# Expert outputs put back by matmuls and summed in SBUF; model dimension in blocks of 512 for the mixture of experts

## What is computed

```
g_val, g_idx = lax.top_k(g_prob, 1)            # one of 4 groups
e_val, e_idx = lax.top_k(e_prob, TOP_K)        # two of its 8 experts
weights = g_val * e_val                        # e_val normalised to sum 1
...
a = jnp.einsum('td,edf->tef', t, w1)
b = jnp.einsum('td,edf->tef', t, w3)
hid = jax.nn.silu(a) * b * cw[:, :, None]
y = jnp.einsum('tef,efd->td', hid, w2)
...
x = x + gt_f * rms_norm(y, g_post_ffn)
```

## Time and profile before

| | |
|---|---|
| median of 3 runs | 1644.57 us (1641.36 to 1647.06) |
| the profiled execution, its own time | 1643.16 us |
| its span in the trace | 1641.3 us |
| first hidden pass starts | 655.94 us |
| last output pass starts | 1604.09 us |
| busy: PE / DVE / ACT / POOL | 72% / 32% / 10% / 8% of the span |
| moved by DMA | 601.0 MB, 366 GB/s over the span |

### The profile page before, as it was taken

How to read it: one execution, slowest core, us unless ns; L and a number is a source line. 1 busy time by engine, 2 the same in 40 slices (tenths; PEclk the granted TensorE clock), 3 DMA queues, 4 the chain that set the end, 5 groups by cost and what they waited for, 6 DMA issues and landing times.

```text
span 1641.3 us, 21098 instructions
## 1 busy us (share of the span) xinstructions
PE 1181.2 (72%) x8541; PEld 597.1 (36%) x8542; DVE 522.5 (32%) x861; ACT 159.5 (10%) x395; POOL 132.4 (8%) x239
## 2 busy tenths in 40 slices
PE   1649999999999997865465465564664669698471
PEld 1538854675445445321122121221221223233120
DVE  4558246565475624212112111121121122223114
ACT  3101121221011011000000000000000000000002
POOL 3000000000010000100100001001001011111102
PEclk8679999899999997978778787787787789899786
DMA  9989869688768977799999999999999998999994
GB/s 301 308 315 380 299 237 354 227 321 312 292 242 320 408 312 308 307 425 433 424 428 426 426 431 425 426 433 423 426 432 425 431 425 341 396 385 407 422 424 189
DMA packets 99964, 601.00 MB, mean 366 GB/s; under 512 B 7736, under 2 KB 18152, under 8 KB 61536
## 3 DMA queue, kind: packets, MB, share of 16 engines
q1 hardware_dynamic: 90352, 571.49, 85.4%
q0 software_dynamic: 7808, 20.85, 4.0%
q10 hardware_dynamic: 1776, 8.28, 1.4%
HBM read 583.28 MB, written 17.32 MB: 366 GB/s over the span
## 4 chain that ended last, share of the span: by engine, by line
PE 52%; DMA 36%; DVE 5%; SPq 4%; issue 2%; ACT 1%; POOL 0%; POOLq 0%; ACTq 0%; DVEq 0%
DMA stream<-in_w 32%; PE ps L586 12%; PE ps L741 11%; PE ps L669 7%; PE ps L758 5%; PE ps L712 5%; PE ps L508 4%; DMA stream<-in_w_ada 3%; PE ps L583 3%; SPq L395 2%; PE ps L537 1%; DVE wk L1075 1%; SPq L400 1%; SPq L455 1%; DVE acc L795 1%
## 5 line engine op out<-in xcount | busy, mean ns | idle before, releaser
L741 PE MATMUL ps<-stream,wk 128*32 128x256 f32 x4608 | 310.7, 437 | 281.8 <-DMA stream<-in_w 280.3
L741 PEld LDWEIGHTS ps<-stream,wk 128*32 128x32 f32 x4608 | 164.0, 126 | 441.6 <-issue 366.7
L1069 DVE COPY wk<-ps 128x512 f32<-128x512 f32 x36 | 24.9, 692 | 778.0 <-PE ps L712 778.0
L586 PE MATMUL ps<-stream 128*128 128x512 f32 x448 | 200.5, 603 | 0.0
L758 PE MATMUL ps<-stream,wk 128*32 128x512 f32 x1152 | 137.3, 618 | 48.8 <-DVE wk L1079 48.6
L712 PE MATMUL ps<-resid,wr 128*32 128x512 f32 x592 | 133.4, 1030 | 2.1 <-DVE wr L1039 2.1
L586 PEld LDWEIGHTS ps<-stream 128*128 128x128 f32 x448 | 85.2, 194 | 100.9 <-issue 100.7
L669 PE MATMUL ps<-stream 128*128 128x512 f32 x256 | 112.8, 603 | 1.3 <-issue 1.3
L508 PE MATMUL ps<-stream 128*128 128x256 f32 x448 | 106.9, 404 | 4.1 <-DMA stream<-in_w_in 2.3
L508 PEld LDWEIGHTS ps<-stream 128*128 128x128 f32 x448 | 91.2, 205 | 18.0 <-DMA stream<-in_w_in 2.7
L1387 POOL COPY wk<-wk 128x512 f32<-128x512 f32 x35 | 21.5, 613 | 803.9 <-ACT wk L1295 803.9
(11 more groups left out here) (236 smaller groups left out, 805.7 us busy)
## 6 DMA issues: line engine op xcount, KB each, us to landing
stream<-in_w SPq DMA_DIRECT2D x128, 2048.0 KB, 25.6
stream<-in_w SPq DMA_DIRECT2D x32, 4096.0 KB, 33.1
stream<-in_w_ada SPq DMA_DIRECT2D x72, 1024.0 KB, 5.7
stream<-in_w_in SPq DMA_DIRECT2D x8, 4096.0 KB, 16.4
stream<-in_w_ada SPq DMA_DIRECT2D x12, 2048.0 KB, 20.4
stream<-in_w_out SPq DMA_DIRECT2D x4, 4096.0 KB, 18.4
stream<-in_w_in SPq DMA_DIRECT2D x3, 3584.0 KB, 23.1
ys<-wk POOLq DMA_DIRECT2D x140, 64.0 KB, 6.3
```

The source lines that it names most:

```text
L586: last = nc.tensor.matmul(bank(fill % 2), hT[:, k, P * half:P * half + P], w[:, k, :], start=(k == 0), stop=(k == KD - 1))
L741: last = nc.tensor.matmul(bank(1)[32 * g:32 * g + 32, 0:256], xe[:, k, :], a13[g // 2][:, k, 256 * (g % 2):256 * (g % 2) + 256], start=(k ...
L1069: V.tensor_copy(xp, bank(0)).then_inc(rows_sb, 1)
```

## The change

**No `ys`.** The writes to HBM, the zeroing, the gather, the gate and sum steps at the end, and POOL's loop are gone. Instead DVE makes from the same 0/1 matrices the gate-weighted ones (`gated`, then `fours`: the 32 columns repeated four times), PE transposes them (two transposes, bank 0), ACT copies them to `spread`, and `add_part(t2, b0)` multiplies `spread` with `ye`: four matmuls with 32 contraction rows each, partition group g of `spread` and `ye` into bank b0+g, all 128 tokens by 512 columns. There are two such calls per tile, one per token half. DVE's `collect` adds the four banks (128 x 2048) to the running sum `ysum[t2]` in SBUF. The sum of tile t-1 is made during tile t; the last one after the loop. Both calls in the loop use banks 4 to 7, so the second waits until DVE has collected the first (`ysum_sb`).

**Order of the model dimension.** For the experts and the router it is split as (g p j): four blocks g of 512, partition p holding dimensions 512g + 4p to 512g + 4p + 3. `pick_rows` now reads x1 in contiguous blocks of 512, `turn_rows` reads every fourth float, and w1 and w3 come in four runs of 8 KB per partition, w3's halves in two. `mod_sums` for m = 3 and 4 takes every 4th float instead of every 16th. The small vectors and router weights are loaded to match: nine more DMAs on POOL's queue at the start.

**`g2b`** is loaded behind the last w2, after the loop, into the buffer of w1.

```diff
-        w1 = a["w1"].rearrange("l e (p k) f -> (l e) p (k f)", p=P)
-        w3 = a["w3"].rearrange("l e (p k) f -> (l e) p (k f)", p=P)
+        w1 = a["w1"].rearrange("l e (g p j) f -> (l e) p g (j f)", g=4, p=P)
+        w3 = a["w3"].rearrange("l e (g p j) f -> (l e) p g (j f)", g=4, p=P)
...
-            sp.wait_ge(g2_out, 16)
-            sp.wait_ge(x1_sq, TT)
-            sp.dma_start(g2b, row_bcast(gdram[1, :, :], D)).then_inc(g2_in, 16)
...
+            sp.wait_ge(g2_out, 16)
+            done = sp.value_load(cums[0:1, NE - 1:NE], min_val=1, max_val=MAX_TILES)
+            sp.wait_ge(ab_ps, done)
+            sp.dma_start(g2b, row_bcast(gdram[1, :, :], D)).then_inc(g2_in, 16)
...
+                    cols = slice(512 * (k // 4) + k % 4, 512 * (k // 4) + 512, 4) if m in (3, 4) else slice(k, D, KD)
...
-                        last = nc.tensor.matmul(bank(0)[32 * g:32 * g + 32, :], pick[:, t2, :], rows[:, t2, 4 * g:4 * g + 4, :], start=(t2 == 0), stop=(t2 == TT - 1))
+                        last = nc.tensor.matmul(bank(0)[32 * g:32 * g + 32, :], pick[:, t2, :], resid[:, t2, 512 * g:512 * g + 512], start=(t2 == 0), stop=(t2 == TT - 1))
...
+            def add_part(t2, b0):
+
+                for g in range(4):
+                    last = nc.tensor.matmul(ps[:, b0 + g, :], spread[32 * g:32 * g + 32, t2, :], ye[32 * g:32 * g + 32, :], start=True, stop=True)
+                last.then_inc(part_ps, 1)
...
-                    last = nc.tensor.transpose(bank(4, 4, P)[:, j, :], xp[:, P * j:P * j + P], ident)
+                    last = nc.tensor.transpose(bank(3, 4, P)[:, j, :], xp[:, j::4], ident)
...
+                        pe.wait_ge(ye_sb, t + 1)
+                        pe.wait_ge(ysum_sb, 2 * t + 2)
+                        add_part(0, 4)
                         pe.wait_ge(pick_sb, t + 2)
                         pick_rows()
...
+                        pe.wait_ge(ysum_sb, 2 * t + 3)
+                        add_part(1, 4)
                         pe.wait_ge(rows_sb, t + 2)
+                        pe.wait_ge(gated_sb, t + 1)
+                        for t2 in range(TT):
+                            last = nc.tensor.transpose(bank(0, 4, P)[:, t2, :], wrf[:, 320 + P * t2:320 + P * t2 + P], ident)
+                        last.then_inc(spread_ps, 1)
                         turn_rows()
...
+            add_part(0, 4)
+            add_part(1, 0)
...
+            def gate_hits():
+
+                return V.tensor_tensor(gated, hit, gates[:, :, :].rearrange("p t j -> p (t j)").unsqueeze(2).to_broadcast((P, 2 * TT, ROWS)), ALU.mult)
+
+            def gate_rows():
+                return V.tensor_tensor(fours, gated[:, 0::2, :].unsqueeze(2).to_broadcast((P, TT, 4, ROWS)),
+                                       gated[:, 1::2, :].unsqueeze(2).to_broadcast((P, TT, 4, ROWS)), ALU.add)
+
+            def collect(t2, b0):
+
+                y4 = ysum[t2].rearrange("p (g n) -> p g n", g=4)
+                V.tensor_tensor(y4, ps[:, b0:b0 + 4, :], y4, ALU.add).then_inc(ysum_sb, 1)
...
-            with pool.Fori(0, total - 1) as t:
-                outputs(t)
-            pool.wait_ge(ye_out, 64 * total)
-            pool.wait_ge(last_out, 64)
-            pool.nop(nofuse=True)
-            for j in range(2 * TT):
-                pool.indirect_dma_start(fin_rows(j), None, ys[:, :], bass.IndirectOffsetOnAxis(ap=slots[:, j:j + 1], axis=0)).then_inc(fin_rows_in[j], 16)
+            pool.wait_ge(x1_sq, TT)
+            pool.memset(ysum[0], 0.0).then_inc(ysum_sb, 1)
             pool.wait_ge(mod_ps, 4)
+            pool.memset(ysum[1], 0.0).then_inc(ysum_sb, 1)
```

More of the change, by code:

```diff
@@ L437, in _ @@
             for j in range(2):
[L438 removed]
+                sp.dma_start(half(blocks(W3[1]), j), half(w3[1], j)).then_inc(w3_in[1][j], 16)
             sp.wait_ge(route_sb, 1)
@@ L1052, in _ @@
             take_mod(5)
+            V.memset(spread, 0.0).then_inc(spread_sb, 1)
             dve.wait_ge(rows_ps, 1)
@@ L1067, in _ @@
                 normed().then_inc(pick_sb, 1)
+                dve.wait_ge(part_ps, 2 * t + 1)
+                dve.wait_ge(ysum_sb, 2 * t + 2)
+                collect(0, 4)
                 dve.wait_ge(rows_ps, t + 2)
@@ L1285, in _ @@
             total = act.value_load(cums[0:1, NE:NE + 1], min_val=NE, max_val=MAX_TILES)
-            act.wait_ge(ye_out, 64)
-            def tile(t):
+            act.wait_ge(ye_sb, 1)
+            with act.Fori(0, total) as t:
                 act.wait_ge(ab_ps, t + 1)
@@ L1291, in tile @@
                 act.wait_ge(h_ps, t + 1)
-                A(eh, bank(2, 2, P)[:, :, 0:64], ACT.Exp, scale=-1.0).then_inc(h_exp, 1)
+                A(eh, bank(1, 4, P)[:, 2:4, 0:64], ACT.Exp, scale=-1.0).then_inc(h_exp, 1)
+                act.wait_ge(spread_ps, t + 1)
+                A(spread, bank(0, 4, P)[:, 0:2, :], ACT.Copy).then_inc(spread_sb, 1)
                 act.wait_ge(ye_ps, t + 1)
-                act.wait_ge(yo_sb, t + 1)
-                A(ye, bank(3), ACT.Copy).then_inc(ye_sb, 1)
-            with act.Fori(0, total - 1) as t:
-                tile(t)
-            tile(total - 1)
-            act.wait_ge(ye_sb, total + 1)
-            act.nop(nofuse=True)
-            for g in range(4):
-                act.dma_start(ys[bass.ds((total - 1) * ROWS, ROWS), 512 * g:512 * g + 512], ye[32 * g:32 * g + 32, :]).then_inc(last_out, 16)
-            def gate(t):
-                act.wait_ge(fin_rows_in[2 * t], 16)
-                A(fin_rows(2 * t), fin_rows(2 * t), ACT.Copy, scale=gates[:, t, 0:1]).then_inc(fin_gate, 1)
-            gate(0)
-            gate(1)
+                A(ye, bank(2), ACT.Copy).then_inc(ye_sb, 1)
             for t in range(TT):
-                act.wait_ge(fin_sum, t + 1)
-                A(stream[:, 2, D * t:D * t + D], fin_rows(2 * t), ACT.Square, accum_out=st[:, 66 + t:67 + t]).then_inc(fin_sq, 1)
+                act.wait_ge(ysum_sb, 2 * total + 3 + t)
+                act.nop(nofuse=True)
+                A(stream[:, 2, D * t:D * t + D], ysum[t], ACT.Square, accum_out=st[:, 66 + t:67 + t]).then_inc(fin_sq, 1)
             for t in range(TT):
@@ L1365, in _ @@
             pool.memset(ye, 0.0).then_inc(ye_sb, 1)
-            pool.wait_ge(ye_sb, 1)
-            spare = ys[NE * ROWS:MAX_TILES * ROWS, :].rearrange("(p r) (g n) -> p (r g) n", p=P, g=4)
-            part = spare.shape[1] // 4
-            for j in range(4):
-                pool.dma_start(spare[:, part * j:part * (j + 1), :], ye.unsqueeze(1).to_broadcast((P, part, 512))).then_inc(ye_out, 16)
             for t in range(TT):
```

124 lines of the change are left out of this document (65 added, 59 removed).

## The result

| | before | after |
|---|---|---|
| median | 1642.96 us (1637.37 to 1647.06, 4 runs) | 1617.01 us (1616.32 to 1617.29, 4 runs) |
| the profiled execution | 1643.16, span 1641.3 | 1617.1, span 1615.3 |

The ratio is 0.9844, with a 95% interval of 0.9813 to 0.9875: 26 us faster.

The account below looks back on a forecast made before the run. Weight loads were taken to bound the experts, except two-tile experts, where PE's tile time is exposed. -8.7 us up to the last output pass and -13.0 in the tail sum to -21.7, giving 1621.5 us, range 1606 to 1636.

Parts of the forecast that it names:

- Before the experts: Start to first hidden pass: nine more small loads, no zeroing and the new mod_sums stride together change nothing, 0 us.
- The gain of up to 7: mod_sums of m = 3 and 4 on PE's path: every 4th float might gain 0 to 7 us; 0 taken.
- The weight stream: Weight loads: batches 0.24 us shorter, 22 of them with one w1 load -5.2, and g2b moved -2.5.
- `g2b`: Its 1 MB load moved from the saturated stream to behind the last w2: -2.5 us.
- One tile: PE's chain up to the output pass: 6.6 us against 6.43, +0.15 on nine exposed tiles, +1.4 in all.
- Rival 2: add_part: row groups overlap only in neighbours, 2.1 us a call, 1635.5 us in all; chance 0.16 shared with another rival.
- Landings and the last batches: Behind the two-tile experts: two weight landings about -0.95 us each, and two more batches -0.5 together.
- The tail: From the last output pass's end to the span's end: 20.5 us instead of 33.6, -13.0.
- Rival 3: add_part: four row groups run one after another, 3.4 us a call, +4.2 on nine tiles, 1661 us; chance 0.06.

Follow-up runs that it names:

- e_one_group: The changed kernel with all four matmuls of each put-back step on the same 32 rows of PE; 1694.4 us, ratio 1.0305 to the kernel before.
- e_order_only: The kernel before with the new order of model dimensions alone, outputs still written to ys and gathered; 1645.9 us, ratio 1.0018.
- e_pick_quads: The changed kernel with the old dimension order, w1 and w3 in 32 KB runs, picking x1 in 16-byte runs; 1604.5 us, ratio 0.9757 to the kernel before.
- e_putback_only: The changed kernel with the old dimension order: outputs put back by PE, strided picking, 32 KB runs; 1619.2 us, ratio 0.9857 to the kernel before.
- e_short_runs: The kernel before with w1 and w3 loaded in four runs of 8 KB per partition instead of one of 32 KB; 1652.3 us, ratio 1.0053.
- e_no_writes: The kernel before without the writes of the experts' outputs to ys inside the expert loop; 1625.3 us, ratio 0.9898.
- e_order_filled: The kernel before with the new dimension order and five unused extra transposes filling PE's rest before the output pass; 1639.2 us, ratio 0.9968.

## Why the prediction was right, step by step

**Before the experts, 0.** Off by 1.7 us. The first hidden pass starts at 654.2 to 656.7 in the seven profiles with the old order of the small vectors and at 657.6 to 659.7 in the four with the new one, so the nine loads or the other column order do cost something; which of the two was not tried. The gain of up to 7 that was kept for `mod_sums` did not come: every 4th float costs PE as much as every 16th in the earlier trace rows (3.63 us for 16 records after as well).

**The weight stream, -7.7 up to the two-tile stretches.** The rate was right: -0.21 per batch against -0.24, since +0.39 for short runs and -0.59 for the writes stood against +0.42 and -0.66. `g2b` was right too (2.3 and 2.5). The measured -10.3 exceeds it by 2.6, and that lies in the first 40 us: from the first to the third hidden pass it is 41.0 us in the profile of before and 38.1 after. 0.7 of it is the first tile (19.0 and 18.3 us to the second hidden pass), which lies on the path too, since w2 of the second expert waits for its output pass; the sum had no term for it. The rest, from the second to the third hidden pass, is 22.0 before and 19.8 after. The eight other profiles, `e_one_group` left out, have 19.1 to 21.5 there, so much of it may be what one execution differs from the next; that is not shown.

**One tile, +0.15 on nine.** `add_part` at 1.1 was right (1.07), and so was the choice of the nearest row: the one that divides by the column groups' ratio. Rival 2's 2.1 did not occur. From the first record of `add_part` to the output pass it is 6.1 us, where 6.6 were reckoned: each hand-over was put about 0.1 too long, `collect` at 2.29 is 2.2 from its start to the next one's, its reading of PSUM was no slower than the earlier trace rows, and the copy to the output pass takes 2.59 instead of 2.76. So the tile is 0.23 shorter rather than 0.15 longer: the term is mis-sized by 0.4, some 3 us on eight tiles. Another 1.7 in this piece is an output pass at the lower clock that the profile of before has on its path and the one after has not, from PE's timeline of before:

```profile
1363.52 5.33 PE L758 MATMUL ps<-stream,wk 128*32 128x512 f32 x32 [1.36 <-DVE wk L1079]
```

The prediction had no term for the clock, and `e_order_only` shows that it was lucky in this: without put-back, the faster picking would have lost by the clock what it gained. The +0.7 of the last tile is the clock as well: its hidden pass took 9.46 us in the profile after and 8.56 in the one before; both start at 1.2 GHz, and the one after stayed there longer.

Two figures in the prediction are slightly off and move its sum by 0.1 at most: `pick_rows` takes 3.5 us from start to start, not 3.4 (the earlier trace rows have 3.61 as its length), and -1.2 + 0.2 + 0.1 for a landing is -0.9.

**Landings and the last batches.** They were put at -0.95 and -0.25 each. The spans from the last tile of a stretch to the landing shrank from 29.0 and 28.3 to 28.2 and 28.1, -0.5 on average. The first (-0.9) is right, the second (-0.2) is not. The two more batches gave -0.9 together instead of -0.5.

**The tail, -13.0.** Measured -12.5, and the chain went as written: ACT's copy, eight matmuls, two collects, gain, residual. What was late is POOL's factor: 2.58 us for one step (1601.33), ending at 1603.9, so the first residual waited 0.54 us. In the tail of before this step took 0.57 us for the first factor and 2.48 for the second; why is open.

**Rival 3** was rightly unlikely, and its +4.2 per tile was right at the full clock (21.11 against 16.80 before), but its 1661 was too low. `e_one_group` gives 1694, 77 more than the changed kernel, where the rival had 40 over the forecast. Missing were the lower clock, some 20 us in the eight tiles and part of the rest, and the first two tiles of the experts, 10.5, for which it had no term.

## What to carry to other kernels

Price a new transfer or matmul by the row that has its shape: w2's 8 KB runs gave the pace of w1 and w3 to 0.03 us per batch, and the column groups gave the row groups. When a rival adds a quarter to a tile, go through the tiles again for those with little slack: behind the second tile of the experts PE waited only 3.1 us for weights, and a tile that is 4.5 us longer uses that up. When a short step makes PE rest, look at the granted clock of what follows before booking the gain, and before changing a layout in HBM for the sake of an operand, try whether the read can go in groups of 16 bytes.

## What the runs showed of the hardware

- Eight records (four float32 matmuls of 32 contraction rows, 512 columns) take 1.07 us on four row groups and 3.63 us on one (after, `e_one_group`).
- DVE adds 128 x 2048 floats in 2.29 us whether one operand lies in PSUM (L1094 after) or both in SBUF (L1095 before).
- PE reads a moving float32 operand in groups of four at a stride of 64 bytes as fast as a contiguous one (16 records in 1.86 and 1.85 us, `e_pick_quads` and after), and single floats at that stride at about half the pace (3.54 from start to start in `e_putback_only`).
- Loads of 4 MB in 8 KB runs instead of one of 32 KB cost 0.2 us more each. The short runs also make the rate flat: slices 17 to 32 stand at 421 to 423 GB/s in `e_short_runs`, with the writes, and at 424 to 433 in `e_no_writes`, with the long runs. With the short runs, the issue of a w3 half takes SP 4.5 to 8.4 us (L464 above) and up to 14.7 elsewhere in the stage. Before, it took 0.3 to 1.4 in the earlier trace rows and 4.6 at most. SP has nothing else to do there, and in the batch shown w3 took 10.0 us for all that.
- In the same place of a tile PE's clock fell to 1.2 GHz in five tiles of eight in which PE had rested 1.26 us ahead of the output pass (`e_order_only`), and in none in which it had rested 0.72 (`e_order_filled`). Rest is not the only thing that goes before a fall: in `e_one_group` the clock fell while PE stood at work nearly all the time, with matmuls of 32 contraction rows on one row group:

```profile
1372.00:1374.00 2.00, 1.75 (x9) 0.86 (x6) 1.97 (x4) 0.28 (x1) 0.00 (x0) 1.00 0.00 0
1374.00:1376.00 2.00, 2.00 (x5) 0.85 (x4) 1.00 (x3) 0.00 (x0) 0.00 (x0) 0.76 0.00 0
1376.00:1378.00 2.00, 2.00 (x5) 0.50 (x4) 0.00 (x0) 0.00 (x0) 0.00 (x0) 0.50 0.00 0
```

The columns are as above; PEclk, third from the right, goes from 1.00 to 0.50.
